# Recurrence gates of an RG-LRU branch: two 64-row tiles on TensorE, eight 64-partition activations on ScalarE

## The reference, cut to what matters

```python
LRU_BLOCKS = 8; LRU_BLOCK_DIM = 64; LRU_WIDTH = 512
def rg_lru(u, conv_w, conv_b, w_rg, b_rg, w_ig, b_ig, lru_L):
    xc = <causal convolution of u, 4 taps, per channel> + conv_b
    xb = xc.reshape(b, s, LRU_BLOCKS, LRU_BLOCK_DIM)
    r = jax.nn.sigmoid(jnp.einsum('bshi,hij->bshj', xb, w_rg).reshape(b, s, c) + b_rg)
    i = jax.nn.sigmoid(jnp.einsum('bshi,hij->bshj', xb, w_ig).reshape(b, s, c) + b_ig)
    log_a = (-LRU_C * r.astype(jnp.float32)) * jax.nn.softplus(-lru_L.astype(jnp.float32))
    a = jnp.exp(log_a)
    mult = jnp.sqrt(-jnp.expm1(2.0 * log_a))
    bx = mult * (i * xc).astype(jnp.float32)
    <h = associative scan of h = a * h + bx over the sequence>
```

## Time and profile before

| | before |
|---|---|
| median of 3 runs | 2349.36 us (2348.14 to 2349.36) |
| profiled execution: time | 2348.64 us |
| profiled execution: span | 2346.8 us |
| TensorE matmul busy | 2312.3 us (99%) |
| VectorE busy | 1444.3 us (62%) |
| ScalarE busy | 1060.1 us (45%) |
| GpSimd (POOL) busy | 1198.6 us (51%) |
| mean granted TensorE clock | 0.999 |

### The profile page before, as it was taken

The page is one execution under the profiler, slowest core; times in us unless marked ns, Lnnn a source line. Parts: engine busy times, 40 slices in busy tenths (PEclk is TensorE's granted clock), DMA queues, the critical chain, the costliest instruction groups (busy, mean ns, idle before and its releaser), DMA issues. The chain is left out here.

```text
span 2346.8 us, 30065 instructions
## 1 busy us (share of the span) xinstructions
PE 2312.3 (99%) x10928; PEld 1905.4 (81%) x10928; DVE 1444.3 (62%) x1682; ACT 1060.1 (45%) x1659; POOL 1198.6 (51%) x819
## 2 busy tenths in 40 slices
PE   8999999999999999999999999999999999999998
PEld 5888888888777888888788888888888777888887
DVE  6566652764497456458887787723854595366366
ACT  4555542443375254331466666632342573255220
POOL 1555543874366344535465565644763555445331
PEclk9999999999999999999999999999999999999999
DMA  5544422123213412364354544322134124312442
GB/s 202 192 156 154 128 106 94 54 81 126 94 59 108 140 54 63 112 251 159 102 161 135 162 153 130 113 90 77 54 118 137 44 62 130 126 54 77 143 171 81
DMA packets 99186, 273.19 MB, mean 116 GB/s; under 512 B 9312, under 2 KB 30944, under 8 KB 98016
## 3 DMA queue, kind: packets, MB, share of 16 engines
q1 hardware_dynamic: 97600, 266.56, 34.4%
q10 hardware_dynamic: 1440, 4.72, 0.6%
HBM read 208.33 MB, written 62.91 MB: 116 GB/s over the span
## 5 line engine op out<-in xcount | busy, mean ns | idle before, releaser
L2166 POOL TENSOR_TENSOR WLS<-SR,WHS 128x512 fp32r<-128x512 f32 x264 | 410.8, 1575 | 158.8 <-ACT WHS L1050 152.4
L724 PE MATMUL J<-XBH,WHS 128*128 128x512 f32 x1152 | 453.6, 394 | 2.6 <-ACT ST L1132 2.0
L726 PE MATMUL J<-XBH,WLS 128*128 128x512 f32 x1152 | 449.3, 390 | 0.0
L725 PE MATMUL J<-XBL,WHS 128*128 128x512 f32 x1152 | 448.9, 390 | 0.0
L724 PE MATMUL J<-XBH,WH 128*128 128x512 f32 x864 | 342.6, 396 | 2.6 <-DVE XBL L1582 1.7
L726 PE MATMUL J<-XBH,WL 128*128 128x512 f32 x864 | 337.0, 390 | 0.0
L725 PE MATMUL J<-XBL,WH 128*128 128x512 f32 x864 | 336.8, 390 | 0.0
L724 PEld LDWEIGHTS J<-XBH,WHS 128*128 128x128 f32 x1152 | 216.4, 188 | 49.6 <-ACT ST L1132 3.2
L726 PEld LDWEIGHTS J<-XBH,WLS 128*128 128x128 f32 x1152 | 216.2, 188 | 45.9
L725 PEld LDWEIGHTS J<-XBL,WHS 128*128 128x128 f32 x1152 | 216.5, 188 | 43.0
L2209 POOL TENSOR_TENSOR REST<-REST,SHARE 128x512 f32<-128x512 f32 (+3 forms) x160 | 168.0, 1051 | 157.0 <-DVE REST L1770 150.4
(11 more groups left out here) (331 smaller groups left out, 4815.3 us busy)
## 6 DMA issues: line engine op xcount, KB each, us to landing
RAW<-w SPq DMA_DIRECT2D x144, 512.0 KB, 3.8
pk_m<-MB SPq DMA_DIRECT2D x56, 512.0 KB, 5.1
MB<-pk_m SPq DMA_DIRECT2D x48, 512.0 KB, 3.9
KC<-pk_k SPq DMA_DIRECT2D x40, 512.0 KB, 5.3
VC<-pk_v SPq DMA_DIRECT2D x40, 512.0 KB, 4.5
BRAW<-w SPq DMA_DIRECT2D x64, 256.0 KB, 5.1
XRAW<-xt SPq DMA_DIRECT2D x8, 1024.0 KB, 13.0
pk_v<-STL SPq DMA_DIRECT2D x16, 512.0 KB, 5.1
```

What stands on the lines that cost most here:

```text
L724: nc.tensor.matmul(to, wh, xh, start=first, stop=True, skip_group_check=True)
L725: nc.tensor.matmul(to, wh, xl, start=False, stop=True, skip_group_check=True)
L726: return nc.tensor.matmul(to, wl, xh, start=False, stop=True, skip_group_check=True)
L2166: low = G_.tensor_tensor(WLS[:, k, :], SR[:, k, :], WHS[:, k, :].bitcast(F32), ALU.subtract)
```

## The change

The two blocks of 64 channels are multiplied apart. WGR has one 128x128 matrix: rows 0 to 63 hold the first block's weights and rows 64 to 127 the second's. In the first block's rows the columns 0 to 63 are r and 64 to 127 are i; in the second block's rows it is the other way round. A call still has four matmuls of 128 columns of weights and 512 columns of data, but each uses 64 rows only: block b = 0 the upper 64 rows, b = 1 the lower ones. Bank BR[b][c] then holds both gates of one block. ScalarE reads 64 partitions at a time, eight activations in place of four, and for i its output lies 64 partitions away from its input. The bias of i is swapped accordingly in the host's layout. The load of WGR is half as large.

```diff
-        WGR = at("WGR", R + 68.25, [2, P])
+        WGR = at("WGR", R + 68.25, [P])
...
-                sp.dma_start(WGR[:].rearrange("p r n -> p (r n)"), wgate[h]).then_inc(gw_in, 16)
+                sp.dma_start(WGR[:], wgate[h]).then_inc(gw_in, 16)
...
-                wait_if(pe, l_sig, 4 * hh)
+                wait_if(pe, l_sig, 8 * hh)
                 if h == 0:
                     pe.wait_ge(mu_done, f_count(half, 1))
-                for r in range(2):
-                    for c in range(NC):
-                        s = slice(c * C, (c + 1) * C)
-                        mm = nc.tensor.matmul(BR[r][c][:], WGR[:, r, :], XC[h % 2][:, s], start=True, stop=True)
+                for c in range(NC):
+                    for b in range(2):
+                        rows = slice(b * P // 2, (b + 1) * P // 2)
+                        mm = nc.tensor.matmul(BR[b][c][:], WGR[rows, :], XC[h % 2][rows, c * C:(c + 1) * C], start=True,
+                                              stop=True)
                     mm.then_inc(gates_done, 1)
...
                 for r, dst in enumerate((LR[h], LI[h])):
-                    act.wait_ge(gates_done, 2 * hh + r + 1)
                     for c in range(NC):
-                        nc.scalar.activation(dst[:, c * C:(c + 1) * C], BR[r][c][:], ACT.Tanh, scale=0.5,
-                                             bias=PRM[:, h, P_BR + r:P_BR + r + 1]).then_inc(l_sig, 1)
+                        act.wait_ge(gates_done, 2 * hh + c + 1)
+                        for b in range(2):
+                            made, to = (slice(q * P // 2, (q + 1) * P // 2) for q in ((b + r) % 2, b))
+                            nc.scalar.activation(dst[to, c * C:(c + 1) * C], BR[b][c][made, :], ACT.Tanh, scale=0.5,
+                                                 bias=PRM[made, h, P_BR + r:P_BR + r + 1]).then_inc(l_sig, 1)
...
-                act.wait_ge(l_sig, 4 * hh + 2)
+                act.wait_ge(l_sig, 8 * hh + 4)
...
-                dve.wait_ge(l_sig, 4 * hh + 4)
+                dve.wait_ge(l_sig, 8 * hh + 8)
...
-            wgate[:, s, r, s] = a[name][0][b::2]
+            s = (b + r) % 2 * 64
+            wgate[:, 64 * b:64 * b + 64, s:s + 64] = a[name][0][b::2]
```

More of the change, by code:

```diff
@@ L2347 @@
     memt = a["mem"][0].reshape(MEM, KD, P).transpose(2, 1, 0)
-    wgate = np.zeros((KB, P, 2, P), np.float32)
+    wgate = np.zeros((KB, P, P), np.float32)
     for r, name in enumerate(("w_rg", "w_ig")):
         for b in range(2):
-            s = slice(64 * b, 64 * b + 64)
-            wgate[:, s, r, s] = a[name][0][b::2]
+            s = (b + r) % 2 * 64
+            wgate[:, 64 * b:64 * b + 64, s:s + 64] = a[name][0][b::2]
     wpool = a["w_pool"][0].transpose(1, 0, 2).reshape(P, HEADS * P)
     cols = [a["conv_w"][0][j] for j in range(TAPS)]
-    cols += [a[n][0] for n in ("conv_b", "b_rg", "b_ig", "lru_L", "pool_scale", "lru_L")]
+    b_ig = a["b_ig"][0].reshape(KB, 2, P // 2)[:, ::-1].reshape(-1)
+    cols += [a["conv_b"][0], a["b_rg"][0], b_ig, a["lru_L"][0], a["pool_scale"][0], a["lru_L"][0]]
     prm = np.stack(cols).reshape(P_ALL, KB, P).transpose(2, 1, 0).reshape(P, KB * P_ALL)
@@ L2362 @@
         cst[:, C_CNT + g * HALO:C_CNT + (g + 1) * HALO] = 1.0 / np.minimum(np.arange(HALO) + 1, w)
-    arrays = {"xt": xt, "xrow": x, "memt": memt, "w8": w8, "w4": w4, "wgate": wgate.reshape(KB, P, 2 * P),
+    arrays = {"xt": xt, "xrow": x, "memt": memt, "w8": w8, "w4": w4, "wgate": wgate,
               "wpool": wpool, "prm": prm, "cst": cst, "ln_g": a["ln_g"][0], "ln_b": a["ln_b"][0]}
```

## The result

The changed kernel takes 2369.8 us (median of 4 runs, 2367.7 to 2375.0) against 2348.9 us before (2348.1 to 2349.4): a ratio of 1.0094, 95% interval 1.0082 to 1.0106. It is slower by 20.9 us. I had forecast slower, 2357, with a range of 2351 to 2368. The way was right; the time lies outside the range, and the loss is two and a half times the 8.1 us of my sum.

What follows compares the result with a forecast made beforehand. TensorE, busy 2312.3 of 2346.8 us, was taken to bound the kernel. Its gain, tile switches and ScalarE's added time summed to +4.06 us a half, +8.1 in all, giving 2357 us, range 2351 to 2368.

Steps and rivals of the forecast that it cites:

- my sum: Whole kernel: +0.14 for call h = 0, +1.34 each for h = 1 to 3, -0.1 a half; +8.1 us in all.
- Where the time is set: From piece 5's end, TensorE's piece 10 waits for ScalarE's copy of piece 7; slack 1.29 us for h = 0, otherwise none.
- Gain of TensorE: Gate matmuls of a call: 1.29 us gained by overlapping tiles, 0.33 us lost to two changes of tile size.
- b1-high starts behind it: Gate matmuls: records run b0-high, b0-low, b1-high, b1-low, so eight fill five slots, 2.15 us a call.
- ScalarE's added time: Gate activations: four more a call, 2.30 us, all new idle time at piece 10 for h = 1, 2, 3.
- I take 0.57 and four more of them: Gate activations: one of 64x512 takes 0.57 us like one of 128x512, so four more cost 2.30 us a call.
- The shift by 64 partitions I cost at nothing: ScalarE's activations for i: writing 64 partitions away from the input adds no time.
- my last rival: Something held covered, VectorE's chain or the clock falling in gaps of some 2.5 us: 2 to 6 us more, 2360 to 2364; 7%.
- The wait for BL: TensorE's wait at each half's end shifts with ScalarE's chain and stays near 1.2 us; 0.1 us off each half.
- VectorE's cover of 0.66 us: VectorE's last sum ends 0.66 us ahead of piece 4; cover grows, but if gone, TensorE's gain becomes waiting.
- Tiles fully side by side, no switch cost: Gate matmuls: gain 1.72 us a call, +2.0 us in all, 2351.4, no measurable change; 22%.
- The tiles run one after the other: Gate matmuls: TensorE gains nothing, +15.8 us, up to +21.4 with switches, 2365 to 2371; 22%.

Runs made afterwards that it cites:

- the copy moved: Changed kernel with ScalarE's copy of piece 7 placed between the four activations for r and the four for i: 2354.9 us.
- ScalarE's half alone: Kernel before with eight tanh activations of 64 partitions a call, unshifted, and its 128-row gate matmuls kept: 2379.4 us.
- the same half in a row: Changed kernel with its eight activations reordered, the two of one half of the partitions behind each other: 2363.5 us.
- filled stalls: Changed kernel with 8 or 14 matmuls that nothing reads put in front of piece 10 in the eight calls: 2362.4 us.
- TensorE's half alone: Changed kernel with four activations of 128 partitions as before, the gates' values mixed up: 2347.2 us.

## Why the prediction was right or wrong

*Where the time is set* was right: the race from piece 5's end to piece 10, in which ScalarE had no slack for h = 1 to 3. TensorE's new idle time stands there, and with the copy moved 15 of the 20.9 us went.

*Gain of TensorE*, -1.29 + 0.33 a call: 0.96 forecast, 1.31 measured. The tiles fill four slots, not five, and the changes of tile size cost 0.41 us, not 0.33. The step that failed is that b0's low record comes next and "b1-high starts behind it": in the trace the first records of both tiles start together, and their second ones together 0.53 us later. The records stood in another order than I had assumed.

*ScalarE's added time*, 2.30 us a call: measured 3.36. This is the error that counts most. The step that failed is "I take 0.57 and four more of them". The 0.57 is the distance between neighbours on the same partitions; the changed kernel alternates between halves, and there it is 0.71. Half of the eight intervals are new activations, but all eight grew. The run with ScalarE's half alone and the one with the same half in a row show it. "The shift by 64 partitions I cost at nothing" holds for the copying itself; a shifted output counts as a change of half. By it the stall at piece 10 is 3.48 us where I had 2.30 new on 0.24, and 2.07 where I had 1.1.

*The sum with these two sizes*: 8 x (3.36 - 2.30) = +8.5, 8 x (0.96 - 1.31) = -2.8, so 8.1 + 8.5 - 2.8 = 13.8 us. The run with filled stalls, which keeps all but the clock, measured 13.9. That these agree to 0.1 is in part luck, as the medians are no surer than some tenths.

*The clock* was in my last rival, 7%, and as "2 to 6 us": it cost about 7 us net. What misled me was that a gap of 1.26 us had cost nothing; the stalls were 2.1 and 3.5 us. With a real stall of 3.5 us it became likely, and since it happens in some calls only, the runs spread over 7 us in place of 1.

*The wait for BL*, which "neither grows nor takes back" what piece 10 lost: right but for 0.1 us without the clock (1.03 with filled stalls; 1.26 before). With TensorE slowed behind the last stall it vanished, and so hid part of the clock's cost.

*VectorE's cover of 0.66 us*: right that it isn't touched by the change, and the condition that I named (gone, it costs what TensorE gains) is half of what kept TensorE's half alone from being worth anything.

*The rivals.* "Tiles fully side by side, no switch cost" was right on the tiles, wrong on the switch cost and on the result. "The tiles run one after the other" gave the nearest number, 2365 to 2371, for a reason that isn't so.

Not settled: why the parts outside the stage differ by up to 2 us between executions even where the clock did not fall there, and what decides, for a stall of a given length, whether the clock falls.

## What to carry to other kernels

Read the engine that waits next, not the one that is fullest: TensorE was 99% busy, and 10.5 us taken off it were worth 1.7, because the chains through ScalarE and VectorE had at most 1.3 us of slack. Splitting an activation by partitions doubled its time here (64 partitions took as long as 128), and alternating the halves took the overlap as well; keep neighbours on the same partitions. And price a stall on TensorE with the clock: the same microsecond can be paid twice.

## What the runs showed of the hardware

- Activations of 512 columns start 0.57 to 0.59 us apart on the same partitions, and 0.69 to 0.71 where input and output, or the output alone, are on others, in neighbours of 64 partitions and from 64 to 128. One of 64 partitions lasts as long as one of 128 (0.68 us). The Trainium skill, "ScalarE: Activation LUTs", "What ACT_TABLE_LOAD costs", says that activations back to back overlap by about 93 ns; that holds in the first case (0.11 us here) and not in the second.
- Two tiles of 64 rows in float32 start 0.01 us apart or together, and both are through in the 0.43 us that one record of 128 rows takes; a call costs 0.41 us beyond its four slots.
- TensorE's clock fell from 2.4 to 1.2 GHz behind 16 of 18 stalls of 3.5 to 3.8 us, 1 of 6 of 2.95, 7 of 16 of 2.1 to 2.5, and behind none of 1.5 or less (stalls at piece 10 and waits for BL, from start to start less 0.23, all profiled executions). It fell mostly for some 8 matmuls, twice for a dozen and more. With the stalls at piece 10 filled with matmuls that nothing needs it stayed at 2.4 GHz throughout.
